# The heads' keys and queries of an mLSTM layer: formed on GpSimd in stage one instead of by block-diagonal projections on TensorE

## What is computed

```python
u = rmsnorm(x, norm_w) @ w_in
x_in, z = u[..., :MLSTM_INNER], u[..., MLSTM_INNER:]
xc_pre, new_buf = causal_conv(x_in, buf, conv_w, conv_b)
xc = jax.nn.silu(xc_pre)
q = headwise(xc, w_q)        # blocks of 4 channels: einsum('btgi,gio->btgo')
k = headwise(xc, w_k)
v = headwise(x_in, w_v)
...
h, C, n, m = mlstm_scan(heads(q), heads(k) / math.sqrt(d), heads(v), ig, lf, C0, n0, m0)
```

## Time and profile before

| | |
|---|---|
| runs, us | 1104.47, 1109.66, 1104.81; median 1104.81 |
| the profiled execution, us | 1102.33, its span 1100.6 |
| granted clock of PE, mean | 0.998 |
| busy: PE, DVE, ACT, POOL | 1077.2, 452.7, 254.4, 155.4 us |
| stage one's last matmul ends | 323.2 us |
| first score matmul of head 0 | 333.9 us |
| first values matmul of heads 1, 2 | 415.4, 482.2 us |

### The profile page before, as it was taken

One profiled execution on the slowest core, in us unless ns is written; L12 is line 12 of the kernel. 1 busy time (PEld: TensorE's weight loads), 2 busy tenths in 40 slices (PEclk: granted clock), 3 DMA queues, 4 the chain that ended last, 5 costly groups with the idle time before them and its releaser, 6 DMA issues.

```text
span 1100.6 us, 12588 instructions
## 1 busy us (share of the span) xinstructions
PE 1077.2 (98%) x4688; PEld 702.4 (64%) x4688; DVE 452.7 (41%) x1075; ACT 254.4 (23%) x525; POOL 155.4 (14%) x240
## 2 busy tenths in 40 slices
PE   7999999999999999999999999999999999999997
PEld 5777777777765354453634677777766666656667
DVE  7433243333347577575665100005243333343215
ACT  3211111111235323232331000010123333242221
POOL 5200010000110324113232011011110101000100
PEclk9999999999999999999999999999999999999999
DMA  6323223322346997979979322122211101202202
GB/s 256 106 82 130 86 81 129 128 81 106 111 144 248 337 372 286 339 278 354 368 303 329 151 75 76 38 77 99 87 54 45 60 20 60 94 17 101 72 24 97
DMA packets 44637, 162.26 MB, mean 147 GB/s; under 512 B 4844, under 2 KB 9196, under 8 KB 35632
## 3 DMA queue, kind: packets, MB, share of 16 engines
q1 hardware_dynamic: 44592, 161.65, 40.5%
HBM read 104.42 MB, written 57.21 MB: 147 GB/s over the span
## 4 chain that ended last, share of the span: by engine, by line
PE 91%; DVE 5%; DMA 2%; ACT 1%; issue 1%; POOL 0%; SPq 0%; DVEq 0%; ACTq 0%; POOLq 0%
PE work_b L633 27%; PE work_a L633 23%; PE work_b L1077 5%; PE work_a L896 5%; PE work_a L790 4%; PE bank L681 3%; PE bank L863 2%; PE work_b L846 2%; DVE arena L1890 2%; PE work_a L1147 2%; PE bank L1122 2%; PE bank L1252 1%; PE work_a L1107 1%; PE work_a L872 1%; PE bank L1125 1%; PE work_a L1220 1%
## 5 line engine op out<-in xcount | busy, mean ns | idle before, releaser
L633 PE MATMUL work_b<-arena,ring 128*128 128x320 f32 x832 | 230.5, 433 | 0.0
L633 PEld LDWEIGHTS work_b<-arena,ring 128*128 128x128 f32 x832 | 155.6, 190 | 61.0
L633 PE MATMUL work_a<-arena,ring 128*128 128x320 f32 x640 | 177.7, 436 | 6.7 <-DMA ring<-in_stream 6.7
L633 PEld LDWEIGHTS work_a<-arena,ring 128*128 128x128 f32 x640 | 121.6, 192 | 55.7 <-DMA ring<-in_stream 6.7
L1890 DVE SCALAR_TENSOR_TENSOR arena<-arena,bank 128x512 f32<-128x512 f32 x128 | 87.1, 743 | 65.1 <-PE bank L863 65.1
L1711 DVE COPY arena<-bank 128x384 f32<-128x384 f32 x64 | 28.5, 486 | 130.1 <-PE bank L681 130.0
L633 PE MATMUL work_a<-xc,ring 128*128 128x320 f32 x256 | 70.4, 434 | 1.9 <-ACT arena L1423 1.3
L633 PE MATMUL work_b<-xc,ring 128*128 128x320 f32 x256 | 69.6, 432 | 0.0
L896 PE MATMUL work_a<-arena 128*128 128x512 f32 x128 | 64.4, 615 | 2.8 <-ACT arena L1405 2.8
L633 PEld LDWEIGHTS work_a<-xc,ring 128*128 128x128 f32 x256 | 48.3, 190 | 23.6 <-ACT arena L1423 2.1
L633 PEld LDWEIGHTS work_b<-xc,ring 128*128 128x128 f32 x256 | 48.6, 190 | 20.3
(11 more groups left out here) (289 smaller groups left out, 1342.2 us busy)
## 6 DMA issues: line engine op xcount, KB each, us to landing
ring<-in_stream SPq DMA_DIRECT2D x66, 512.0 KB, 3.5
arena<-in_c SPq DMA_DIRECT2D x32, 1024.0 KB, 8.2
out_s_c<-arena SPq DMA_DIRECT2D x32, 1024.0 KB, 5.6
v_scratch<-arena SPq DMA_DIRECT2D x16, 320.0 KB, 4.7
k_scratch<-arena SPq DMA_DIRECT2D x16, 320.0 KB, 4.4
z_scratch<-arena SPq DMA_DIRECT2D x16, 320.0 KB, 4.6
arena<-k_scratch SPq DMA_DIRECT2D x4, 1280.0 KB, 12.9
arena<-z_scratch SPq DMA_DIRECT2D x4, 1280.0 KB, 9.8
```

The lines of the kernel that those rows point to most:

```text
L633: done = mm(halves(buf)[:, a, :], lhs, rhs[:, a * HALF:(a + 1) * HALF], start=first, stop=last)
```

## The change

Keys and queries become a sum over the four rotations of a block: out = w0 * x + w1 * x(turned by 1) + w2 * x(turned by 2) + w3 * x(turned by 3), where partition p of a turned row holds the channel (p + r) modulo 4 of p's own block, and w_r is one number per partition. POOL has no way across partitions, so the turning goes through DRAM: xcs is written twice, into rows 0 to 3 and 4 to 7 of each block in rows_scratch, and read back three times from row r + 1. POOL then scales the three turned rows and adds them to the unturned one (mix), for all 640 tokens with the folded key weights (wk_s) and for the 128 stream tokens with the query weights (wq_r). The result, 768 columns per chunk, is mixed; SP stores it in mix_scratch, and each head loads its four chunks into k_t, whose last 128 columns are the queries. project_head, its matmuls and evictions, and head_basis go. Scores(h + 1, 0) stand where project_head(h + 1) stood, before step 7. Each one-column copy to carry in mix carries a wait for POOL's own results. Buffers of stage two move (h_t and zh lie over x_rot and mixed, and wait for the last mixed store), and the c0 loads move behind the wait for stage_left and head 0's mixed keys.

```diff
+            def stage_a(j, end=False):
                 for s in range(SLOTS):
                     load_weight((j + 1) * SLOTS + s, s, A.fill[s % 2])
                 for s in range(2):
+                    sp.wait_ge(xcs_ready, c.next(xcs_ready))
+                    for first in (0, 4):
+                        sp.dma_start(rows_dram[s, :, first:first + 4], xcs[s]).then_inc(rows_out, c.up(rows_out, 16))
                     for ready, out, slot, dram in ((vs_ready, v_out, vs, v_dram), (ks_ready, k_out, ks, k_dram),
                                                    (zs_ready, z_out, zs, z_dram)):
...
-            c.rounds(NI // 2, stage_a)
+                sp.wait_ge(rows_out, c.all(rows_out, step=16))
+                for s in range(2):
+                    for r in range(3):
+                        op = sp.dma_start(x_rot[s][:, r], rows_dram[s, :, r + 1:r + 5])
+                        op.then_inc(rows_in, c.up(rows_in, 16))
+                if not end:
+                    store_mixed(j)
+
+            def store_mixed(j):
+                for s in range(2):
+                    sp.wait_ge(mix_ready, c.next(mix_ready))
+                    sp.dma_start(mix_dram[j * 2 + s], mixed[s]).then_inc(mix_out, c.up(mix_out, 16))
+
+            c.rounds(NI // 2 - 1, stage_a)
+            stage_a(NI // 2 - 1, end=True)
...
+            sp.wait_ge(stage_left, 4)
+            load_mixed(0)
...
             load_kv(0)
+            store_mixed(NI // 2 - 1)
...
+                    if n == 3 and h + 1 < HEADS:
+                        sp.wait_ge(score_mm, TT * (h + 1))
+                        sp.wait_ge(qm_ready, h + 1)
+                        load_mixed(h + 1)
...
                 if h + 1 < HEADS:
-                    project_head(h + 1)
+                    scores(h + 1, 0)
                     step(h, 7, t0 + 4)
-                    for t in range(TT):
+                    for t in range(1, TT):
                         scores(h + 1, t)
...
+            def mix(n, s):
+                at = iter(range(8))
+
+                def after_own():
+                    pool.wait_ge(pool_own, c.all(pool_own))
+                    k = next(at)
+                    op = g.tensor_copy(carry[:, n, k:k + 1], coef[s][:, 0:1])
+                    op.then_inc(pool_own, c.up(pool_own))
+
+                parts = [(mixed[s][:, T:MIX], q_terms[s], own, 4), (mixed[s][:, 0:T], x_rot[s], whole, 0)]
+                for dst, terms, src, w in parts:
+                    after_own()
+                    for r in range(1, 4):
+                        op = g.tensor_scalar(terms[:, r - 1], x_rot[s][:, r - 1, src], coef[s][:, w + r:w + r + 1], None, ALU.mult)
+                        op.then_inc(pool_own, c.up(pool_own))
+                for r in range(1, 4):
+                    after_own()
+                    for dst, terms, src, w in parts:
+                        raised = mix_ready if r == 3 and w == 0 else pool_own
+                        g.tensor_tensor(dst, dst, terms[:, r - 1], ALU.add).then_inc(raised, c.up(raised))
...
                     pool.wait_ge(xcs_ready, c.next(xcs_ready))
-                    g.tensor_copy(xc[:, n, :], xcs[s]).then_inc(xc_kept, c.up(xc_kept))
-            c.rounds(NI // 2, stage_a)
-            leave(c)
+                    g.tensor_copy(xc[:, n, :], xcs[s]).then_inc(pool_own, c.up(pool_own))
+                    op = g.tensor_scalar(mixed[s][:, 0:T], xcs[s], coef[s][:, 0:1], None, ALU.mult)
+                    op.then_inc(pool_own, c.up(pool_own))
+                    op = g.tensor_scalar(mixed[s][:, T:MIX], xcs[s][:, own], coef[s][:, 4:5], None, ALU.mult)
+                    op.then_inc(xc_kept, c.up(xc_kept))
+                if end:
+                    leave(c)
+                c.skip(mix_out, 2, step=16)
+                c.skip(rows_in, 6, step=16)
+                pool.wait_ge(rows_in, c.all(rows_in, step=16))
...
+                mix(j * 2, 0)
+                mix(j * 2 + 1, 1)
```

More of the change, by code:

```diff
@@ L288, in program @@
         zs = [take(T) for _ in range(2)]
+        mixed, q_terms = [None, take(MIX)], [None, take(3, P)]
+        carry = take(NI, 5)
+        coef = [take(8) for _ in range(2)]
+        fx = take(T)
         a_end = top[0]
         assert a_end <= c_at, a_end
+        top[0] = KD * T
+        x_rot = [take(3, T) for _ in range(2)]
+        mixed[0], q_terms[0] = take(MIX), take(3, P)
+        assert top[0] <= 2 * KD * T
         top[0] = c_at
@@ L296, in program @@
         vh = take(KH, NP, P)
-        v_s = [take(KH, P) for _ in range(2)]
+        v_s = [take(KH, P), None]
+        h_t = take(KH, T)
+        zh = take(KH, T)
+        k_t = take(KH, MIX)
+        v_s[1] = take(KH, P)
         kz_at = top[0]
         kz = [take(2, KH, P) for _ in range(2)]
[L300 to L305, removed]
         pt = take(DW)
         qm = take(KH, 2, P)
+        h_at = top[0]
         mbw = take(T + P)
@@ L419, in score_bank, with q_t @@
             return banks[t % len(banks)][:, 0:WID[t]]
[L421 to L434, removed]
-            return PROJ * h + (KH if h else 0) + j + 1
-        def query_place(h):
-            return PROJ * h + (KH if h else PROJ)
-        def key_kept(h, j):
-            before = sum(vector_keeps(h, n) == vector_keeps(h, j) for n in range(j + 1))
-            return KH * h + before if vector_keeps(h, j) else (KH + 1) * h + before + (1 if h else 0)
+        def q_t(q):
+            return k_t[:, q, T:MIX]
         out_after = {0: (0, 1), 1: (2,), 3: (3,), 4: (4,), 5: (5,)}
@@ L483, in _ @@
             first_weights(3)
-            for dst, name in ((rowc[0:HEADS], "rows"), (n_t, "n0"), (bmask, "bmask"), (parity, "parity"), (later, "later"), (wq_rep, "wq_rep")):
+            for dst, name in ((rowc[0:HEADS], "rows"), (n_t, "n0"), (bmask, "bmask"), (parity, "parity"), (later, "later"), (turned_w, "turned_w")):
                 sp.dma_start(dst, i[name]).then_inc(misc_in, c.up(misc_in, 16))
@@ L509, in _ @@
                 load_c(s)
-            sp.wait_ge(stage_left, 4)
             scratch_written(sp)
-            def chunks(dram, h, part):
-                return dram[h * KH:(h + 1) * KH, :, part].rearrange("c p n -> p c n")
             def load_kv(h):
@@ L811, in small_sums @@
                    start=True, stop=True, skip_group_check=True).then_inc(small_mm, 1)
-            project_head(0)
-            for t in range(2):
+            for t in range(3):
                 scores(0, t)
@@ L828, in _ @@
             op.then_inc(G.bfill[0], c.up(G.bfill[0]))
-            for t in range(2, TT):
+            for t in range(3, TT):
                 scores(0, t)
@@ L1310, in stage_a @@
                         act.wait_ge(xc_kept, due)
+                    if (due := c.all(rows_out, step=16)) is not None:
+                        act.wait_ge(rows_out, due)
                     act.wait_ge(conv_done, c.next(conv_done))
@@ L1316, in stage_a @@
                         c.skip(q)
+                c.skip(rows_out, 4, step=16)
             c.rounds(NI // 2, stage_a)
```

167 lines of the change are left out of this document (64 added, 103 removed).

## The result

The changed kernel takes 1243.87 us (median of 4 runs, 1241.60 to 1245.30) where the kernel before takes 1104.64 (1104.04 to 1109.66): a ratio of 1.126, interval 1.123 to 1.129. The prediction was 1186 us with a range to 1232. The sign, the place and the order of the events were right; the size was not, by 57.9 us.

The account below looks back on a forecast made before the run. TensorE, 98% busy, bounds the kernel, and SP's queue holds back its slot 0 weights behind GpSimd's mix: 1102.3 + 58 (stalls) + 13 (clock) + 25 (handover) - 12 (stage two) = 1186 us, range 1136 to 1232.

Parts of the forecast that it names:

- 58 + 13: Stage one's loop: +58 us for six stalls at slot 0, +13 us for slow groups behind them.
- What bounds, and where it breaks: Stage one: TensorE bounds, 98% busy; slot 0's weights, with 23.3 us of slack, come late behind SP's wait for GpSimd.
- The round trip: Stage one, slot 0 to slot 0: 11.7 + 8.2 + 24 + 1.0 + 3.9 = 48.8 us against 39.1.
- I price it as a copy: GpSimd's mix in stage one: scalings at 0.79 us wide and 0.37 narrow, 3.5 us a chunk.
- my upper bound, the addition's price: GpSimd's mix in stage one: scalings priced as additions with full holding up, 29 us, +88 us in all.
- What I added for VectorE's and GpSimd's hold-up: Stage one's mix: 2.6 us for VectorE's convolution beside it, bringing the mix of two chunks to 24 us.
- The clock: Stage one: the group behind each stall runs 2.2 us longer, six times, +13 us.
- Rival 3: Stage one: whole group behind each stall at 1.2 GHz, 8.8 us extra in six rounds, 1226 us; chance 0.11.
- The handover: End of stage one: first score 20 us later plus 5 us for later loads and mixing, +25 us.
- Stage two: Later heads: projections go, 17.9 us at most, less late keys and queue load; 4 us a transition, -12 us.
- rival 2: Stage two gives nothing back, as loads end later by as much as TensorE saves; 1198 us, chance 0.20.
- The wait for late keys: Stage two's later heads: values and keys land late, a wait of 2 us replacing part of the projections.

Follow-up runs that it names:

- The order turned round: Changed kernel with SP storing a round's mixed rows one round later, behind the next round's ring loads; 1182.3 us.
- the fillers: Changed kernel plus 28 idle matmuls in TensorE's pause before the slot 0 weights, in rounds 1 to 7 only; 1232.19 us.
- the last two runs: Kernel mixing on VectorE, its last pair mixed on GpSimd beside heads 0 and 1: 1100.13 us; the same plus 11 idle matmuls before head 0: 1097.45 us.
- the last run: The 1100.13 us kernel with 11 idle matmuls in TensorE's wait for head 0's row vectors; 1097.45 us, ratio 0.9941.

## Why the prediction was wrong

The median is 57.9 us over the forecast. By the profiled runs about 43 of it are from the loop of stage one (114.1 where 58 + 13 stood), 9 from the way to head 0's values (27.3 + 7.1 where 25 stood), and 6 from the rest (a gain of 6.0 where 12 stood).

- **What bounds, and where it breaks.** Right: slot 0 of the next round stood in SP's queue behind GpSimd, six times. The order turned round removes the ring waits, and so confirms it.
- **The round trip**, by its own steps, measured from 219.59 to 277.93: to the last gate store 13.9 us (predicted 11.7; the difference is the slow group); to the start of the mixing 9.8 (8.2, a term 1.6 too small); the mixing 29.7 (24); stores and issue 1.2 (1.0); landing 3.9 (3.9). In all 58.3, against 48.8 and 2.2 for the clock. Of the 7.3 us a round that are missing, 5.7 are the mixing.
- **The step that failed** is the price of the six wide scalings of a pair, "I price it as a copy", 0.79 us. They take 1.89, and the six narrow ones 0.64 where 0.37 stood: 8.2 us a pair that the sum did not have. Both runs that touch the scalings alone say so: as copies the round is 49.0 us, without them 40.1. From the copies' 20.6 us, six times 1.13 and six times 0.34 more (the 128-column form takes 0.64, the copy 0.29) give 29.4, where 29.7 were measured. Even my upper bound, the addition's price, was too low, because I took for granted that one input is cheaper than two. The Trainium skill (GPSIMD Engine Reference, Engine selection) had said the same, one-input work roughly at line rate; the trace holds against it for this form, a multiplication by one coefficient per partition: 1.89 us for 640 columns, 2.9 ns a column, where the copy takes 0.72.
- **What I added for VectorE's and GpSimd's hold-up** and the handoffs was too much, by about 2.5 us a pair: 24 and the 8.2 make 32.2, and 29.7 were measured. The effect is there: below, a 128-column step of the convolution that takes 0.34 us elsewhere takes 1.63, and the addition beside it 2.01 where 1.51 is the mean.

```profile
198.71 2.01 POOL L2150 TENSOR_TENSOR arena<-arena 128x640 f32<-128x640 f32 x1
...
199.25 1.63 DVE L1656 SCALAR_TENSOR_TENSOR arena<-arena,vec 128x128 f32<-128x128 f32 x1
```

- **The clock**: 14.4 us measured on the six groups, 11.7 given back by the fillers, 13 predicted. The group on slot 0 took 8.8 us at full clock and 10.6 to 11.8 behind gaps of 15 to 17 us. It began at the lower of the two levels and ended at the upper: in the group that starts at 219.59 the weight loads follow each other every 0.53 us up to 224.54, and the other 22 take 5.84 us, 0.27 each.

```profile
224.02 0.34 PEld L644 LDWEIGHTS work_a<-arena,ring 128*128 128x128 f32 x1 [0.20 <-issue]
224.54 5.84 PEld L644 LDWEIGHTS work_a<-arena,ring 128*128 128x128 f32 x22 [0.18 <-issue]
```

  The six groups behind the shorter gaps of the run with copies, 5.8 to 8.0 us, took as much, 10.5 to 11.9. The Trainium skill (TensorE: Matmul & The Clock Gate, Why this matters for your kernels) says that idle gaps bring the clock down; the trace agrees. Rival 3, which had it stay down for the whole group, would have needed 8.8 us more a round; 2.4 were measured.
- **The handover**: the forecast's 25 us were 20 up to the first score and 5 for what follows it in head 0. The first score came 27.3 us later and head 0's values another 7.1. The first is mostly the same step again: GpSimd ended its mixing at W + 40.2 where the forecast had W + 34, and left at about W + 51 instead of W + 45. PE waited 19.7 us for that leave and 15.6 for the mixed rows, and had 8 us of projections less to do. The second I had not priced: some 5 of the 7.1 us are products at the lower level of the clock, 2.05 to 2.08 us each, and 1.6 a wait for VectorE. The forecast put the lower clock in stage one alone.
- **Stage two**: 12 us of gain predicted. From the first score to the end 1.1 were lost, which is rival 2's total but not its mechanism: 7.1 went before head 0's values, as just said, and the heads did become 6.5 us shorter. Of PE's work in the three heads some 16 us went, near the 17.9 at most of the forecast. Against that stand 4.9 us more of waiting and 4.6 of products at the lower clock, 3.0 at the start of head 0 and 1.7 behind one of these waits. The wait for late keys that the forecast named is there, 1.8 to 2.0 us in each of heads 1 to 3: in front of its first update PE waits for ScalarE, and ScalarE for the keys' load.

```profile
564.21 1.33 ACT L1358 ACTIVATE arena<-arena 128x512 f32<-128x512 f32 x2 [4.18 <-DMA arena<-k_scratch]
...
566.71 1.14 PE L840 MATMUL bank<-arena 32*128 32x512 f32 x8 [1.80 <-ACT arena L1381]
```
- **The range** ended at 1232. With the mixing at its upper bound (+88), the clock and the handover as forecast and nothing back from stage two the sum is 1228, still short of 1243.9; it would have taken the handover's or the clock's upper bound as well. The range counted on such bounds not coming together, and two of them nearly did: the mixing took 29.7 us where its bound was 29, and the way to head 0's values 34.4 where its bound was 35.

## What to carry to other kernels

Price an operation on GpSimd from a row with the same operation and operands, and where there is none, give the bound a margin above the dearest row: a scaling by a column of coefficients cost 2.6 copies here. Before a wait is put into a queue that issues loads, ask which engine it stands for and how long its work may grow until the load behind it comes late; here there was room for some 13 us of mixing, and it took 30. And work that hides beside a chain is free: head 0's projections gave nothing when they went. Moved into pauses that VectorE and GpSimd had anyway, the same mixing left the kernel 0.4% faster than the one before, and 0.6% with PE's pause filled.

## What the chip showed that I had not expected

- GpSimd, 640 columns of fp32: copy 0.72 us, addition 1.51, multiplication by a coefficient per partition 1.89. VectorE: the same multiplication 0.55, multiplied and added in one 0.88.
- A pause of PE of 5.05 us in front of head 0 was enough for the lower level of the clock in what follows (2.07 us instead of 1.12); with that filled, a pause of 1.10 us further on, among short products, was followed by it too (2.06). The length of a pause alone does not decide: in front of the gate rows PE paused 1.20 us in the kernel before and in the last two runs, and the products behind it took 1.25 us twice and 2.29 in the last run. Idle matmuls in the pause give it back for as long as they fill it.
